# First block: gates, projections and half of w_out set between the steps of both attentions

## What is computed

```python
def first_block(...):
    h = h + hybrid_mixer(rms_norm(h, attn_norm_g), w_in, fox_forget_b, ret_norm_g, w_out, valid)
    h = h + conv_ffn(rms_norm(h, ffn_norm_g), w_up, conv_w, conv_b, w_down, valid)
    return rms_norm(h, final_norm_g)[:, PREFIX:]

def hybrid_mixer(h, w_in, forget_b, ret_norm_g, w_out, valid):
    rq, rk, rv, rg, fq, fk, fv, ff = split(h @ w_in)
    o_r = retention(rotary(rq), rotary(rk), rv)            # 4 heads, decay instead of softmax
    o_r = o_r * rsqrt(mean(o_r * o_r) + EPS) * ret_norm_g * silu(rg)
    log_f = log_sigmoid(ff + forget_b)
    o_f = forgetting_attention(fq, fk, fv, log_f)          # 8 heads, softmax with a cumulated bias
    return concatenate([o_r, o_f]) @ w_out
```

## Time and profile before

| | |
|---|---|
| median of 3 runs | 2998.38 us (2997.67 to 3006.76) |
| the profiled execution | 3003.84 us |
| its span | 3002.5 us |
| mean granted TensorE clock | 0.963 of full speed |
| TensorE busy | 2639.8 us (88%) |
| VectorE busy | 1573.3 us (52%) |
| ScalarE busy | 651.6 us (22%) |

### The profile page before, as it was taken

How to read it: one execution, slowest core, us unless ns; L and a number is a source line. 1 busy time by engine, 2 the same in 40 slices (tenths; PEclk the granted TensorE clock), 3 DMA queues, 4 the chain that set the end, 5 groups by cost and what they waited for, 6 DMA issues and landing times.

```text
span 3002.5 us, 23370 instructions
## 1 busy us (share of the span) xinstructions
PE 2639.8 (88%) x8074; PEld 1387.7 (46%) x8074; DVE 1573.3 (52%) x3510; ACT 651.6 (22%) x1573; POOL 547.8 (18%) x523
## 2 busy tenths in 40 slices
PE   8998999999998999999999988889877777777776
PEld 3684446666444444356657533445432323232222
DVE  1106335443106991266634676647675676758554
ACT  2114220001001002156511112212121221222111
POOL 0000000000000000000001343334434434434332
PEclk9997899999999999999999998999999899999999
DMA  3220023343221221000236999999999999999997
GB/s 137 99 84 1 22 84 140 140 168 128 90 77 64 84 79 49 14 1 1 81 117 253 380 377 384 398 392 411 411 419 404 387 420 420 420 420 420 420 420 313
DMA packets 87156, 685.25 MB, mean 228 GB/s; under 512 B 9960, under 2 KB 10600, under 8 KB 12800
## 3 DMA queue, kind: packets, MB, share of 16 engines
q0 software_dynamic: 73728, 536.90, 44.0%
q1 hardware_dynamic: 11264, 141.82, 12.4%
q10 hardware_dynamic: 2048, 5.03, 0.5%
HBM read 681.62 MB, written 2.10 MB: 228 GB/s over the span
## 4 chain that ended last, share of the span: by engine, by line
PE 64%; DMA 23%; DVE 8%; ACT 3%; issue 1%; POOL 0%; ACTq 0%; DVEq 0%
PE psum L345 34%; DMA weights<-in_experts,expert 12%; PE psum L896 12%; DMA slot<-in_experts,expert 11%; PE psum L829 3%; PE psum L738 3%; PE psum L683 2%; PE psum L796 2%; DVE slot L1835 2%; PE psum L760 1%; DVE weights L1835 1%; PE psum L811 1%; PE psum L746 1%; ACT spare_row L1292 1%; PE psum L519 1%
## 5 line engine op out<-in xcount | busy, mean ns | idle before, releaser
L896 PE MATMUL psum<-slot,spare_row 128*128 128x512 f32 x1096 | 518.6, 618 | 123.0 <-ACT spare_row L1292 120.6
L896 PE MATMUL psum<-weights,spare_row 128*128 128x512 f32 x952 | 457.2, 625 | 152.4 <-ACT spare_row L1292 145.8
L1835 DVE CUSTOM_DVE_ANT_0 slot<-slot,hT 128x1024 f32<-128x1024 f32 x274 | 333.6, 1222 | 198.2 <-DMA slot<-in_experts,expert 196.6
L345 PE MATMUL psum<-xnT,weights 128*128 128x257 f32 (+2 forms) x1568 | 423.8, 432 | 2.8 <-DVE xnT L1341 2.8
L896 PEld LDWEIGHTS psum<-slot,spare_row 128*128 128x128 f32 x1096 | 207.0, 196 | 410.9 <-issue 211.9
L1889 POOL DMA_INDIRECT weights<-in_experts,expert x238 | 253.2, 1064 | 767.6 <-PE psum L896 399.2
L1835 DVE CUSTOM_DVE_ANT_0 weights<-weights,hT 128x1024 f32<-128x1024 f32 x238 | 290.0, 1223 | 182.8 <-DMA weights<-in_experts,expert 181.8
L896 PEld LDWEIGHTS psum<-weights,spare_row 128*128 128x128 f32 x952 | 180.1, 198 | 416.9 <-ACT spare_row L1292 215.1
L1889 POOL DMA_INDIRECT slot<-in_experts,expert x274 | 291.4, 1064 | 418.6 <-PE psum L896 404.0
L345 PEld LDWEIGHTS psum<-xnT,weights 128*128 128x128 f32 x1568 | 298.8, 191 | 118.5 <-issue 82.2
L1287 ACT ACTIVATE coef<-hidden 128x2 f32<-128x2 f32 (+1 forms) x257 | 52.2, 203 | 1004.5 <-DVE hidden L1835 1004.5
(11 more groups left out here) (320 smaller groups left out, 2534.0 us busy)
## 6 DMA issues: line engine op xcount, KB each, us to landing
weights<-in_w_mod SPq DMA_DIRECT2D x12, 2048.0 KB, 8.7
weights<-in_w_up SPq DMA_DIRECT2D x11, 2048.0 KB, 7.7
weights<-in_w_in SPq DMA_DIRECT2D x8, 2048.0 KB, 8.7
weights<-in_w_pq SPq DMA_DIRECT2D x8, 2048.0 KB, 10.4
weights<-in_w_out SPq DMA_DIRECT2D x6, 2048.0 KB, 8.7
weights<-in_w_in_t SPq DMA_DIRECT2D x4, 2048.0 KB, 10.7
weights<-in_w_down SPq DMA_DIRECT2D x4, 2048.0 KB, 7.8
weights<-in_w_o_mla SPq DMA_DIRECT2D x4, 2048.0 KB, 8.7
```

Of the source, the lines that this page charges most:

```text
L345: last = pe.matmul(out, lhsT, rhs, start=start and n == 0, stop=stop and n == len(pairs) - 1)
L896: last = pe.matmul(acc.pair[:, half, :], k.diags[pick % 8], k.slots[slot][:, D + half * 512:D + (half + 1) * 512], start=h0 == 0 and j == ...
L1835: ins = dve.tensor_tensor_reduce(slot[:, 0:D], slot[:, 0:D], k.h2[:, i, :], 1.0, 0.0, ALU.mult, ALU.add, hid[:, j:j + 1])
```

## The change

- **Norm tile by tile.** All engines now take the first norm one tile after another, and the `rv` projection of a tile follows two transposes later. ScalarE loads its table for the square root ahead of the data.
- **Constants** other than `ident` and `cols` are issued by SyncE, behind the first two weight units. The four rotation tables have four buffers.
- **Rotated rows.** The swap of row j stands behind the projection of row j + 1; the forget gate stands before the last swap.
- **Pieces beside attention.** Gates (4 pieces) and half of the forgetting rows (4) stand in turn with the ten steps of retention; forgetting values (5), the other half of the rows (4) and the first half of w_out's contraction (10 pieces of 4 matmuls) stand in turn with the 23 steps of fox, as `BESIDE_RET` and `BESIDE_FOX` say. The same order is on ScalarE and VectorE. Six score tiles of a retention head lie in two takes of a pair.
- **Second half of w_out** follows, tile by tile.
- **PSUM split.** In this stage a take names its pairs: dense pieces 0 and 1 beside retention, 0 beside fox; retention 2 and 3; fox scores and bias 1 and 2, transposes 3, values 0.
- **Ring.** `scoresT[1]` moves from `xnT` to the third weight buffer, so two buffers (0, 1) serve the mixer. From w_up on the order is 2, 0, 1, and up u comes before mod u.

The core of the diff:

```diff
+RET_STEPS = ("s0", "s1", "v0", "s2", "v1 n0", "s3", "v2 n1", "v3", "n2", "n3")
+BESIDE_RET = (1, 1, 1, 1, 1, 1, 1, 1)
+BESIDE_FOX = (1, 1, 1, 1, 1, 2, 2, 1, 1) + 10 * (1,)
...
+    def bank(self, n, among):
+        if among:
+            at = self.own.get(among, 0)
+            at += at % n
+            self.own[among] = at + n
+            return 2 * among[at // 2 % len(among)] + at % 2
...
     def mod_unit(self, m):
-        return 8 + 2 * m
+        return self.first_ffn + min(1 + 2 * m, 2 * (NF // 2))
...
+    def beside_dense(self, dense, sparse, steps):
+        for piece, n in zip(dense, steps):
+            piece()
+            for _ in range(n):
+                next(sparse)
...
-    k.scoresT = [scoresT0[:], k.xnT[:, 0:NT + 1, :]]
+    k.scoresT = [scoresT0[:], k.wring[2][:, 0:(NT + 1) * NK].rearrange("p (j n) -> p j n", n=NK)]
...
+    def first_stage():
+        pe.wait_ge(s.ld_const, 32)
+        k.ring.order = [0, 1]
+        unit = None
+        for i in range(NT + 2):
+            if i <= NT:
+                pe.wait_ge(s.xn1, i + 1)
+                if i < NT:
+                    turn(("xnT1", i), k.xn1[:, i, :])
+                else:
+                    turn_meta(("xnT1", NT), k.xnm1[:])
+            if i:
+                if unit is None:
+                    unit, w = weights(KC, 512)
+                rows("rv", i - 1, w)
...
         for j in range(4):
             u = project(("rqk", j), w, j * P, k.xnT)
+            if j:
+                swap(j - 1)
         k.ring_done[unit] = u.full[-1]
+        project("forget", k.wff, 0, k.xnT, FH)
+        swap(3)
...
         def transposes(c):
-            u = take(("fox_t", c), reads=1 if i == NT else 2, n=2)
+            u = take(("fox_t", c), reads=1 if i == NT else 2, n=2 if i == NT - 1 else 1, among=(3,))
...
+    def mixer():
+        k.ring.order, k.ring.at = [2], 0
+        k.lent1 = k.ring.turn(load=False)
+        k.ring.order, k.ring.at = [0, 1], 0
+        attention1 = retention()
+        k.beside_dense(gates1() + forgetting_rows(0, (0, 1)), attention1, BESIDE_RET)
+        for _ in attention1:
+            pass
+        attention1 = fox()
+        k.beside_dense(forgetting_values() + forgetting_rows(1, (0,)) + first_out(), attention1, BESIDE_FOX)
+        for _ in attention1:
+            pass
...
+    def first_out():
+        def one(half, i, n, at):
+            if not held:
+                pe.wait_ge(s.ret_mixed, RH)
+                held.extend(weights(KC, 512) for _ in range(2))
+            unit, w = held[half]
+            u = take(("out", 0, half, i), among=(0,))
+            chain(u.pair[0:n, 0, :], [(k.mixedT[:, c, at:at + n], w[:, c, :]) for c in range(4)]).then_inc(u.fill())
...
+    def second_out():
+        for i, n, at in tiles()[1:] + tiles()[:1]:
+            for half in range(2):
...
+                for c in range(4, KC):
...
+                k.ring_done[unit] = u.full[-1]
+        k.ring.order, k.ring.at = [2, 0, 1], 0
...
     def ffn_up():
-        k.ring.turn()
+        k.first_ffn = len(k.ring.turns)
         for u_ in range(NF // 2):
             unit, w = weights(KC, 512)
+            k.ring.turn()
...
-            k.ring.turn()
             mod_finish(u_)
+        k.ring.turn()
...
     weights("w_in_v", 0)
+    weights("w_in_t", 0)
+    for dst, name in ((k.swap1, "swap1"), (k.wff, "w_ff"), (k.fb, "fox_b"), (k.sel, "sel")):
+        sp.dma_start(dst[:], A[name]).then_inc(s.ld_mixer, 16)
...
+    ring[0] += 1
+    weights("w_in_t", 1)
+    weights("w_in_t", 2)
     weights("w_in_v", 1)
...
+    weights("w_in_t", 3)
     for unit in range(2):
         weights("w_out", unit)
-    weights("w_mod", 0)
     for unit in range(NF // 2):
         weights("w_up", unit)
-        weights("w_mod", unit + 1)
+        weights("w_mod", unit)
+    weights("w_mod", NF // 2)
```

More of the change, by code:

```diff
@@ L398, in in_projection @@
             u = project(("rqk", j), w, j * P, k.xnT)
-            k.ring_done[unit] = u.full[-1]
-            v = take(("swap", j), n=2)
-            pe.wait_ge(*u.free)
-            for a in range(2):
-                last = pe.matmul(v.pair[:, a, 0:HALF], k.swap1[:], k.raw[j % 2][:, a * HALF:(a + 1) * HALF], start=True, stop=True)
-            last.then_inc(v.fill())
-        unit, w = weights(KC, 512)
-        for j in range(RH):
-            u = project(("rg", j), w, j * P, k.xnT)
-        k.ring_done[unit] = u.full[-1]
@@ L411, in in_projection, with dense_pieces, one @@
[L411 to L415, removed]
+            if j:
+                swap(j - 1)
+        k.ring_done[unit] = u.full[-1]
+        project("forget", k.wff, 0, k.xnT, FH)
+        swap(3)
+    def dense_pieces(n, piece):
+        held = []
+        def one(j):
+            if not held:
+                held.extend(weights(KC, 512))
+            u = piece(j, held[1])
+            k.ring_done[held[0]] = u.full[-1]
+        return [lambda j=j: one(j) for j in range(n)]
@@ L418, in scores @@
         def scores(h):
[L419 to L430, removed]
+            rows_ = slice((h % 2) * RDK, (h % 2) * RDK + RDK)
@@ new lines, in scores, with block @@
+            q, key = k.rqk[rows_, h // 2, :], k.rqk[rows_, 2 + h // 2, :]
+            if h % 2 == 0:
+                pe.wait_ge(s.rqk, 3 + h // 2)
+            def block(out, j, a, b):
+                n, at = (P, META + j * P) if j < NT else (META, 0)
+                return pe.matmul(out, key[:, at:at + n], q[:, a:b], start=True, stop=True)
+            u = take(("ret_s", h, 0), reads=3, n=2, among=(2, 3))
+            block(u.pair[:, 0, :], 0, META, NK)
+            block(u.pair[:, 1, 0:384], 1, META + P, NK)
@@ L452, in retention @@
         pe.wait_ge(s.ones, 2)
[L453 to L460, removed]
+        for step in RET_STEPS:
+            for what, h in step:
+                {"s": scores, "v": values, "n": norm}[what](h)
+            yield
     def fox():
         def bias(h):
-            u = take(("fox_b", h), n=2)
+            u = take(("fox_b", h), n=2, among=(1, 2))
             for a in range(2):
@@ L904, in peer @@
                 ps.held.discard(acc.at)
-    norm1()
-    in_projection()
-    retention()
-    fox()
-    out_projection()
+    first_stage()
+    rotated()
+    mixer()
+    second_out()
     ffn_up()
```

354 lines of the change are left out of this document (204 added, 150 removed).

## The result

The changed kernel takes 3019.55 us (median of 8 runs, 3012.48 to 3023.03); the kernel before, run beside it, 3002.32 (2997.67 to 3008.03). The ratio is 1.0056 with an interval of 1.0042 to 1.0069: slower by 17 us, a small change but clear of the noise. The profiled execution has a span of 3016.5 us, 14.0 more than that of before.

What follows compares the result with a forecast made beforehand. It took TensorE between 0 and about 780 us to bound the kernel; its terms, -3.8 + 2.8 + 22 + 1.4 - 22.5 - 7.9 = -8.0 us, gave 3006.4 us against the 2998.38 median, range 2983 to 3020.

Steps and rivals of the forecast that it cites:

- the forecast case: Whole kernel: the summed terms hold, 8.0 us longer, 3006.4 us; chance 0.52, own range 2998 to 3015.
- the second rival: The ten w_out steps and steps without a piece: the attention chain paces them, 12 to 15 us more, 3020; chance 0.14.
- first stage: First norm, constants and first projection: earlier start, but transposes behind it and a low clock; -3.8 us (-0.5 to -6).
- rotated rows: Rotated projections: 3.6 us of idle time behind ScalarE's copies goes, one 0.85 us wait comes; +2.8 us (2 to 3.6).
- attentions beside dense work: Both attentions: of 47.7 us idle or slow clock, new waits together keep 25.7; +22 us (+10 to +38).
- second half of w_out: Rest of w_out, before the feed-forward: started warm, it saves slow clock; +1.4 us (0 to 2).
- feed-forward, mod banks: Feed-forward steps 1 to 3: TensorE waits 5.4 us for a mod bank, plus 2.1 slow clock each; -22.5 us.
- entry to the down-projection: First down matmul: w_down asked for late, start 7.2 us later, slow clock more, a 1.4 us wait gone; -7.9 us.
- 2.1 of slow clock behind it: Allowance for lost clock behind a new TensorE wait: 2.1 us, between bounds 0 and 3.9.
- The first rival: Second tile of feed-forward steps 1 to 3: the wait does not show; 2983.9, or 2976 without part 7; chance 0.22.
- the third: At all new waits: the clock does not fall at 5 us, six terms of 2.1 vanish, 2993.8; chance 0.12.
- The signs: First gate piece to w_out's second half some 263 us, clock over 0.95; feed-forward near 405; named waits there and before w_out, down-projection.

Runs made afterwards that it cites:

- e1: The changed kernel with only the old order of units restored (mod u+1 asked for behind up u): 2986.71 us, ratio 0.9937 to the kernel before.
- e2: The kernel before with only the new order of units, up u before mod u: 3037.42 us, ratio 1.0113.
- e3: The changed kernel with VectorE emptying a step's mod banks before it sums the next unit: 2992.03 us, ratio 0.9969 to the kernel before.
- h1: e1 with all dense pieces ahead of retention and fox instead of in turn with their steps: 3021.62 us, ratio 1.0065 to the kernel before.
- f1: e1 with w_out's two units taken one by one, the second only by the sixth piece: 2975.63 us, ratio 0.9921 to the kernel before.
- f5: f1 with one fox step behind each of the nineteen pieces, none doubled: 2976.31 us, ratio 0.9914 to the kernel before.
- g1: e1 with w_out's units taken singly, all transposes before the first projection, and second-norm scaling between the additions: 2976.97 us, ratio 0.9912 to the kernel before.

## Why the prediction was right, point by point

It said 3006.4 within 2983 to 3020, with 0.40 for slower; 3019.55 is slower and inside by 0.45 us. That is a narrow hit with luck in it: the forecast case had its own range up to 3015, and the 3020 was there for the second rival, whose mechanism did not come. The predicted loss was 8.0 us, the measured one 17.2, over twice as much; 3.9 us of the distance to 3006.4 come from the median of three runs it was set on (2998.38, against 3002.32 of eight). Its terms against the changed kernel's profile, in us of gain:

| term | predicted | measured |
|---|---|---|
| first stage | -3.8 | -2.2 |
| rotated rows | +2.8 | +3.6 |
| attentions beside dense work | +22 | +14.0 |
| second half of w_out | +1.4 | +2.0 |
| feed-forward, mod banks | -22.5 | -23.2 |
| entry to the down-projection | -7.9 | -10.1 |
| sum | -8.0 | -15.9 |

**Both losing mechanisms were right in place and price.** 5.4 us for each mod wait was 5.2 (15.6 for three), and 2.1 of slow clock behind it was 2.6 behind the first; 7.2 for w_down was 7.2. e1, e2 and e3 show cause and size each way. The first rival (the feed-forward wait does not show) and the third (no fall of the clock) are refuted.

**The two small terms** came near for partly other reasons. The first projection started at 14.82 (15.4 said) and lost 1.7 us to the low clock (2.1 said). In the rotated rows the wait for VectorE's multiply came as put (0.96 us, 0.85 said); the stretch is still 3.6 us shorter, since TensorE's busy time in it also fell by 0.9.

**The attention term was mis-sized by 8 us.** Its waits were, if anything, too dear: TensorE idled 18.4 us in the fox stretch, where the sum had 23. The bank waits came as put: 2.6 us for the bias, 2.8 behind values, 4.5 for the second transposes (5.7 said), 5.1 for w_out. What failed is "2.1 of slow clock behind it", counted once there:

```profile
185.20:230.30 45.10, 44.23 (x142) 19.24 (x141) 19.32 (x56) 13.10 (x36) 0.00 (x0) 1.00 0.08 27
230.30:237.10 6.80, 6.80 (x22) 5.15 (x21) 1.69 (x6) 2.10 (x5) 0.00 (x0) 0.53 0.38 159
...
250.80:254.20 3.40, 3.40 (x10) 2.62 (x10) 0.00 (x0) 0.00 (x0) 0.00 (x0) 0.56 0.00 0
...
264.50:267.90 3.40, 3.40 (x10) 2.69 (x10) 2.14 (x9) 1.97 (x6) 0.00 (x0) 0.57 0.02 7
...
278.10:281.50 3.40, 3.40 (x13) 2.82 (x12) 1.69 (x6) 1.10 (x3) 0.00 (x0) 0.56 0.00 0
...
291.80:298.60 6.80, 3.48 (x5) 0.68 (x6) 0.00 (x0) 0.00 (x0) 0.00 (x0) 0.53 0.28 118
298.60:365.70 67.10, 60.89 (x279) 27.77 (x277) 30.05 (x116) 19.47 (x62) 0.00 (x0) 1.00 0.00 1
```

Five stretches at half clock hold 20.5 us of matmuls, some 10 lost where 2.1 were put: 8 us. Why the clock fell in the four ahead of the w_out wait is not shown.

The other error is hidden, since it cancels with the waits that were too dear. The estimate of 83.6 us of full-speed work was right for the kernel before, where six stretches at half clock, among them these, hold 59.7 us of busy time:

```profile
252.40:269.40 17.00, 11.45 (x42) 6.58 (x42) 14.68 (x37) 7.83 (x24) 0.00 (x0) 0.51 0.00 0
...
276.30:293.30 17.00, 16.12 (x66) 8.33 (x68) 8.26 (x45) 6.76 (x25) 0.00 (x0) 0.52 0.01 1
```

112.98 less half of 59.7 is 83.1. But the changed stage holds more than these 83.1 and the 154 of pieces: TensorE is busy for 90.36 + 162.10 us, less 10 of slow clock makes 242, some 5 more than 237. What they are is open.

So the 14.0 us won in this stage are not idle time filled. TensorE idled 18.3 us in the attentions before and 18.8 in the stage now. Slow clock cost 29.9 us before and 10 now: **what the change as a whole won in this stage was the clock**, and 5 us of it went into the longer work. By the prediction's sum idle time would have risen to 23.6 us and slow clock fallen to 2.1; it had the direction and not the sizes. Against h1, the same layout without turns, the turns save both: TensorE idles 43.3 us there from the first gate piece to the end of fox, and 19.2 in e1, and slow clock costs 28 us there and 10 in e1.

**The entry to the down-projection** cost 2.2 us more than put. The granted clock was low for 10.2 us, but from 755.5, while TensorE was still idle until 760.19; the 64 matmuls behind the wait took 30.47 us against 27.71 before, so 2.8 were lost where 2.1 were put. And the wait for the context norm, which was to vanish, is still 1.39 us: VectorE begins the norm only behind TensorE's own mod matmuls of that step (790.50), so it moved with them.

**The second rival** (the chain paces every w_out step) was right about a worse attention stage but not about the reason: in the w_out part (298.6 to 365.7) TensorE was busy for 60.89 of 67.1 us at full clock.

**The signs** that the prediction named came: the stretch with the pieces lasted 271.3 us (263 said) at a mean clock of 0.96, the feed-forward began at 409.9 (near 405 said), and the waits of 5.1, three times 5.2 and 7.2 us stood where they were to stand.

## What to carry over

When the order of a ring of buffers is changed, write down for each unit whose place it takes, and when its reader wants it: with three buffers one swap of two lines had each of eleven loads asked for a step later, just when its reader was ready (ten of w_mod and the first of w_down). A late engine costs only through what it holds; here it was one PSUM bank, and emptying it first took back 23 us of 33. Setting dense work between attention's steps is worth some 38 us against the same layout without turns, but that layout without them (h1) is 0.65% slower than the kernel before, and the two together won 14 us in this stage. TensorE idles there as long as before; what went is slow clock, so count idle time and slow clock apart before such a change. The best versions here, f1, f5 and g1, keep the turns: 0.991 to 0.992 of the kernel before.

## What the runs showed of the hardware

The granted clock fell at 230.3 us for 6.8 us although TensorE had been busy for 44.23 of the 45.1 us before, with no single wait over 0.9 us. In the changed kernel it fell thirteen times up to 960 us: behind the waits of 5 to 7 us in the feed-forward, for w_out and for w_down, and behind several waits of about 1 us among small matmuls in fox. In e1 and f1, which do the same work up to 230 us, it stayed low there for 3.4 us. So what a wait costs in slow clock depends on its surroundings and on the execution.

A low stretch is not lost work in full. The three waits of 5 us in the feed-forward each came with 6.8 us at half clock, but the clock fell before the wait had ended (at 458.6 for the first, which ended at 460.10), and the 48 matmuls behind it took 2.6 us longer (16.65 against 14.05), where the prediction had put 2.1. Behind the 7.2 us for w_down it was 2.8 us, of 10.2 at half clock.
